# Which engine adds the weighted v rows while the later bodies attend

## The reference

```python
def block(args):
    xt, et, gt = args
    act = jax.nn.gelu(jnp.einsum('td,thkd->thk', xt, u[et]), approximate=False)
    return jnp.einsum('thk,thkd->td', gt * act, v[et])

x = x + hybrid_mixer(rmsnorm(x, norm_mix), ...)          # MLA, RG-LRU and differential heads
x = x + memory_cross_attention(rmsnorm(x, norm_cross), ...)
x = x + peer_ffn(rmsnorm(x, norm_ffn), ...)              # block() above, for all tokens
out = rmsnorm(x, norm_final)
```

## Time and profile before

| | |
|---|---|
| median of 3 runs | 3480.52 us (3478.77 to 3481.6) |
| profiled execution, span | 3488.4 us |
| PE busy | 2948.9 us, 85% |
| VectorE (DVE) busy | 2349.6 us, 67% |
| GpSimd (POOL) busy | 2015.7 us, 58% |
| ScalarE (ACT) busy | 812.5 us, 23% |
| DMA | 1345.09 MB, mean 386 GB/s |

### The profile page before, as it was taken

One profiled execution on the slowest core, in us unless ns is written; L12 is line 12 of the kernel. 1 busy time (PEld: TensorE's weight loads), 2 busy tenths in 40 slices (PEclk: granted clock), 3 DMA queues, 4 the chain that ended last, 5 costly groups with the idle time before them and its releaser, 6 DMA issues.

```text
span 3488.4 us, 34790 instructions
## 1 busy us (share of the span) xinstructions
PE 2948.9 (85%) x10984; PEld 1651.9 (47%) x10984; DVE 2349.6 (67%) x5893; ACT 812.5 (23%) x1915; POOL 2015.7 (58%) x2085
## 2 busy tenths in 40 slices
PE   7876898888988898889997899888998889976675
PEld 6465455544545355534554456444564445522222
DVE  6229846886588765886578765886648865596555
ACT  3111411132211421133211322114221232211111
POOL 1004755666566765666565655665556655477775
PEclk9898999999999999999999999998999999999998
DMA  7788999999999999999999999999999999999998
GB/s 279 277 274 313 408 409 409 408 409 409 409 407 406 394 409 409 408 407 382 409 409 408 392 356 409 409 409 348 359 409 409 409 355 342 385 404 410 409 409 347
DMA packets 386971, 1345.09 MB, mean 386 GB/s; under 512 B 41762, under 2 KB 44834, under 8 KB 386148
## 3 DMA queue, kind: packets, MB, share of 16 engines
q0 software_dynamic: 294912, 1073.87, 78.1%
q1 hardware_dynamic: 90724, 264.79, 20.0%
q10 hardware_dynamic: 1152, 4.19, 0.3%
HBM read 1332.99 MB, written 35.39 MB: 392 GB/s over the span
## 4 chain that ended last, share of the span: by engine, by line
PE 38%; DMA 30%; DVE 15%; POOL 9%; issue 6%; ACT 3%; SPq 1%; DVEq 0%; POOLq 0%; ACTq 0%
PE ps_sum L1267 18%; DMA rows<-in_peer_u,ids_u 13%; DMA rows<-in_peer_v,ids_v 10%; PE ps_p L999 5%; POOL rows L824 5%; POOL rows L810 4%; DVE rows L2052 4%; PE ps_s L1181 4%; DMA rows<-in_peer_v,ids_u 3%; DMA w_ring<-packed 3%; PE ps_s L1118 2%; PE ps_p L1126 2%; DVE feat_b L1935 1%; DVE feat_b L1931 1%; PE ps_s L1114 1%
## 5 line engine op out<-in xcount | busy, mean ns | idle before, releaser
L1267 PE MATMUL ps_sum<-rows,diag 128*128 128x512 f32 x3548 | 1727.6, 629 | 267.1 <-DMA rows<-in_peer_v,ids_v 141.4
L2052 DVE CUSTOM_DVE_ANT_0 rows<-h_cur,rows 128x1024 f32<-128x1024 f32 x1024 | 1226.8, 1220 | 496.3 <-DMA rows<-in_peer_u,ids_u 483.3
L810 POOL DMA_INDIRECT rows<-in_peer_u,ids_u x1024 | 1012.3, 989 | 702.0 <-issue 483.3
L1267 PEld LDWEIGHTS ps_sum<-rows,diag 128*128 128x128 f32 x3548 | 671.0, 200 | 1155.7 <-issue 1005.7
L824 POOL DMA_INDIRECT rows<-in_peer_v,ids_v x512 | 490.3, 958 | 433.8 <-PE ps_sum L1267 277.6
L824 POOL DMA_INDIRECT rows<-in_peer_v,ids_u x512 | 498.2, 973 | 284.7 <-PE ps_sum L1267 144.2
L1528 ACT ACTIVATE diag<-ident,acts 128x128 f32<-128x128 f32 x887 | 324.7, 394 | 1049.4 <-PE ps_sum L1267 750.1
L999 PE MATMUL ps_p<-hT,w_ring 128*128 128x128 f32 x2944 | 358.7, 282 | 28.8 <-DMA w_ring<-packed 15.3
L999 PEld LDWEIGHTS ps_p<-hT,w_ring 128*128 128x128 f32 x2944 | 353.0, 198 | 61.2 <-issue 39.7
L1834 DVE CUSTOM_DVE_ANT_0 e<-ps_s,bias_t 128x256 f32<-128x256 f32 (+6 forms) x96 | 74.2, 773 | 176.3 <-PE ps_s L1118 73.7
L2074 DVE SCALAR_TENSOR_TENSOR x_cur<-rows,acts,x_cur 128x1024 f32<-128x1024 f32 x137 | 175.6, 1282 | 7.4 <-DMA rows<-in_peer_v,ids_v 7.3
(11 more groups left out here) (288 smaller groups left out, 2376.2 us busy)
## 6 DMA issues: line engine op xcount, KB each, us to landing
w_ring<-packed SPq DMA_DIRECT2D x343, 512.0 KB
w_ring<-in_wstream SPq DMA_DIRECT2D x65, 512.0 KB
packed<-in_wstream SPq DMA_DIRECT2D x49, 512.0 KB, 8.2
rows<-in_peer_u,ids_u POOLq DMA_INDIRECT x1024, 14.9
rows<-in_peer_v,ids_u POOLq DMA_INDIRECT x512, 12.6
rows<-in_peer_v,ids_v POOLq DMA_INDIRECT x512, 19.3
bias_rows<-rows SPq DMA_DIRECT2D x5, 1024.0 KB, 12.1
bias_t<-in_x SPq DMA_DIRECT2D x8, 512.0 KB, 7.9
```

What stands on the lines that cost most here:

```text
L810: pool.indirect_dma_start(u_rows[:, slot, :], None, peer_u, bass.IndirectOffsetOnAxis(ap=ids_u[:, j:j + 1], axis=0)).then_inc(u_landed[slo ...
L1267: ins = pe.matmul(ps_sum[:, c * 512:(c + 1) * 512], diag[:, n % 4, :], v_rows[:, slot, c * 512:(c + 1) * 512], start=(j == 0), stop=(n == ...
L2052: dve.tensor_tensor_reduce(row, h_cur[:, :], row, 1.0, 0.0, ALU.mult, ALU.add, dots[:, p:p + 1]).then_inc(u_used, 1)
```

## The change

on_vector gets a table of shares for the rows 10 to 45 of a block, by the body in which the block is retrieved: every fourth row in body 4, every third in body 5, every second in bodies 6 and 7. All other rows keep the rule of every eighth. Nothing else is edited; the order of pieces and positions stays as it is.

```diff
+ATTEND_SHARE = {4: 4, 5: 3, 6: 2, 7: 2}
+ATTEND_FIRST, ATTEND_LAST = 10, 46
+
+
 def on_vector(b, j):
 
-    return j % SHARE == SHARE - 1 or (b == NB - 1 and j >= TAIL and j % 2)
+    share = ATTEND_SHARE.get(b + 1, SHARE) if ATTEND_FIRST <= j < ATTEND_LAST else SHARE
+    return j % share == share - 1 or (b == NB - 1 and j >= TAIL and j % 2)
```

## The result

The changed kernel takes 3509.3 us (median of four runs, 3504.8 to 3511.6) where the kernel before takes 3480.7: a ratio of 1.0081, interval 1.0065 to 1.0097. A gain of 27 us was forecast, a loss of 29 us was measured. The kernel before ran beside each experiment, at 3482.6 to 3485.9 us there, so the experiments are told by their ratios to it.

A forecast was written before the change was run, and what follows sets the result against it. PE was taken as the bound by share, with softmax hand-overs among PE, VectorE and ScalarE limiting the gain: bodies 4 to 7 give 3 + 5 + 9 + 10 = 27 us, so 3453.5 us from 3480.5, range 3430 to 3470.

The forecast's parts named there:

- What bounds the kernel: Gathers at about 409 GB/s, except dips at positions 23 to 59 of bodies 4 to 7, with PE busy 89 to 91%.
- The 70 us of unused DMA time: Bodies 4 to 7, positions 23 to 59: 5.5, 15.0, 23.6 and 26.0 us, the most the change can win.
- PE's freed time: Bodies 4 to 7: 41 row sums leave PE, 1.95 us each on average, 1.85 at full clock, 80 us.
- The clock rival: Fewer rows on PE mean more gaps; 40 us more at the low clock cost 20, giving 3474 us; chance 6%.
- The walk: Body 6 followed by VectorE's maxima and combines: about 9 us of its 23.6 won, then carried to bodies 4, 5, 7.
- maximum 4: Body 6's score maximum at 2419.89, counted from 0: VectorE becomes late by 0.5 us, so it comes 1.3 earlier.
- Its last sum, 7.4 and 1.0: Body 6: 7.4 us won at the join and at most 1.0 us in mix_out, taken as about 9 us.
- The adds ahead of position 30: Body 6, new VectorE adds at positions 24 and 26; the walk begins behind them and gives them no price.
- VectorE's adds: Bodies 4 to 7: 41 more adds on VectorE at about 1.2 us each, 49 us.
- The release: Slot release for GpSimd moves from PE's row count to VectorE's; costed at nothing, between 1.9 us gain and 1.2 loss a body.
- Gather issues: Rival: if GpSimd limits ring refills, each add stretches an issue 0.46 us, 19 us of the 27: 3472; chance 7%.
- The adds in series: Rival: every new add makes the maximum behind it late, nothing won, 49 us added: 3529; chance 4%.

The follow-up runs named there:

- the table from row 17 on: The changed kernel with its table of shares starting at row 17, so no extra adds at positions 23 to 29: 3494.8 us, ratio 1.0035.
- the filled kernel of before: The kernel before, plus 40 short products with zeros on PE in its waits for ScalarE's copy, bodies 4 to 7: 3474.2 us, ratio 0.9971.

## Why the prediction was wrong

Its direction was wrong, and the time outside the range. By its steps:

- *What bounds the kernel.* Right: the dips, their place, the DMA rate outside them. The 70 us of unused DMA time were there; none of it was won, and after the change it is about 85 us by the same reckoning.
- *PE's freed time, 1.85 to 1.95 us a row, 80 us.* This step failed. It takes the clock as given and counts each removed row as time won. The counts came out, the time didn't: PE's busy time is between 4 us more and 14 us less, not 80 less, the clock fell from 0.941 to 0.926 (medians of the timed runs), and with nothing but a lighter PE the kernel lost 0.2 to 0.3%.
- *The clock rival.* The right mechanism, mis-sized and given 6%. It took 40 us more of low-clock time at a cost of 20; there were 162 us over the run between the profiles, about 110 by the medians, and about 100 in the stretches, a cost of 81, 55 and 50. Its sign, a granted clock under 0.85, came in bodies 6 and 7 (0.81 and 0.83), while body 6 took 144 us at 331 GB/s, not 131 at over 360. It was also held to end at no change at worst, because only its cost against a gain of 27 was reckoned. The walk itself made VectorE's chain the longer one at maximum 4 and between combines, so it had PE wait there; each such wait is a gap of the kind that stands in the earlier trace rows ahead of a sum of 3.31 us. The walk and the rival should have been one sum.
- *The walk.* Its first part came out, its second didn't. The first maximum of body 6 before, and after it the first maximum, maximum 4 and the four combines of the changed kernel:

```profile
2381.69 1.09 DVE L1834 CUSTOM_DVE_ANT_0 e<-ps_s,bias_t 128x896 f32<-128x896 f32 x1 [0.92 <-PE ps_s L1114]
```

```profile
2389.06 1.09 DVE L1839 CUSTOM_DVE_ANT_0 e<-ps_s,bias_t 128x896 f32<-128x896 f32 x1 [2.80 <-PE ps_s L1119]
...
2425.64 1.08 DVE L1839 CUSTOM_DVE_ANT_0 e<-ps_s,bias_t 128x896 f32<-128x896 f32 x1
...
2433.78 1.15 DVE L1872 SCALAR_TENSOR_TENSOR e<-e,small 128x896 f32<-128x896 f32 x1
...
2447.94 1.15 DVE L1872 SCALAR_TENSOR_TENSOR e<-e,small 128x896 f32<-128x896 f32 x1
...
2466.12 1.15 DVE L1872 SCALAR_TENSOR_TENSOR e<-e,small 128x896 f32<-128x896 f32 x1
...
2479.69 1.15 DVE L1872 SCALAR_TENSOR_TENSOR e<-e,small 128x896 f32<-128x896 f32 x1
```

  From the first maximum to the first combine 49.6 us became 44.7: 4.9 won, for the 5 that the walk has, and VectorE is late ahead of maximum 4, as it says. Between the combines the walk has 13.0, 14.6 and 12.2 us; they took 14.2, 18.2 and 13.6, where before they took 13.8, 15.95 and 11.6. There PE's pieces, taken at 1.7 to 1.9 us, ran at up to twice that. Both are single executions with clock dips of their own, so how near the first part comes is in part luck. Its last sum, 7.4 and 1.0, is 8.4 and was taken as 9.
- *The adds ahead of position 30.* This step failed too: the walk began behind them, without a price. Against the start of the stretch (2371 and 2376), body 6's first maximum comes 2.4 us later than before (2381.69 and 2389.06 above), and the six rows that the table from row 17 on puts back were worth 16 us.
- *VectorE's adds.* Well sized as work: 53 us for 49. As time they cost 7 us when PE keeps its load.
- *The release.* Costed at nothing; nothing measured where VectorE has no extra adds (1.0003). In the changed kernel GpSimd does wait for them in body 6, 12.3 us on top of a wait for PE that stayed at 27.0 (27.3 in the earlier trace rows):

```profile
POOL rows L829 <- PE ps_sum L1272: 27.0, 8, 7.7
...
POOL rows L829 <- DVE x_cur L2079: 12.3, 5, 7.9
```

  The same loads with the release left to PE stand at 1.0071 for the changed kernel's 1.0081, so what the release costs there is inside the intervals.
- *Gather issues.* Costed at nothing in the forecast, 19 us in the rival. The mean issue of a u row is 989 ns before and after, of the first half's v rows 973 and 984: the stretching by the adds is seen in single pairs and comes to some 7 us of issue time over the run, on an engine that is busy 58%.
- *The adds in series.* The only slower case named, and not what happened: its price is that of the adds, which alone cost 0.2%.

## What to carry to other kernels

Taking work off TensorE is not free where TensorE hands work to and fro with other engines: read the granted clock of the stretch, and count each removed piece as a gap, before its time is counted as won. Where the gaps are known waits, a short product that has no effect, placed in the gap itself, can be worth more than the removed work; at the removed rows' old places such products held the clock and won nothing. Compare clocks over several runs, not over two profiles. And a walk along the hand-overs must start where the first edited instruction stands.

## What the runs showed of the hardware

- Some 56 us net of TensorE work taken away and nothing added, and the kernel is 0.3% slower: the clock is 0.926 for 0.941 (medians of the timed runs; 0.925 for 0.947 in the profiles), and TensorE is busy 2961.0 us, where unchanged work takes 2949 to 2967.
- In the attention of body 6 before, PE's longest gap was 2.72 us, and the window behind it had a granted clock of 0.57. The Trainium skill ("TensorE: Matmul & The Clock Gate", Part 1) describes an idle TensorE that is put back to the lower clock. The trace agrees at three places: the lower level stands behind waits of 2.72 us and of 3.25 and 2.58 us in the changed kernel. It also stands behind waits of 0.58 and 0.66 us there, while behind 1.85 us in the filled kernel of before a row sum took 1.88 us, its full-clock time.
- The clock can be held from outside the chain: 40 short products in waits that were there anyway are worth 0.8% on the changed kernel and 0.3% on the one before.
